# Expert stage of a two-block transformer kernel: rows turned inside gate/up, gate and residual folded into the scatter sums, last norm read from PSUM

## The reference, cut to what matters

```python
def hier_moe(h, ...):                       # t: 256 x 1024, routed to 2 of 16 experts
    def expert_step(acc, xs):
        w1e, w3e, w2e, ge = xs              # 1024x512, 1024x512, 512x1024, gate of each token
        y = (jax.nn.silu(t @ w1e) * (t @ w3e)) @ w2e
        return acc + ge[:, None] * y, None
...
x_lat = x_lat + g2 * hier_moe(h2_l, ...)    # g2: 1024 values
...
rmsnorm(x_lat, final_g)                     # y * rsqrt(mean(y*y) + eps) * g
```

## Time and profile before

| | |
|---|---|
| median of 3 runs | 1057.99 us |
| profiled execution, first to last instruction (span) | 1055.0 us |
| outside the span, against the median | 3.0 us |
| PE busy | 988.6 us (94%) |
| DVE busy | 525.0 us (50%) |
| ACT busy | 423.2 us (40%) |
| granted TensorE clock, mean over the span | 0.978 |
| bytes moved by DMA | 246.60 MB |

### The profile page before, as it was taken

One profiled execution on the slowest core, in us unless ns is written; L12 is line 12 of the kernel. 1 busy time (PEld: TensorE's weight loads), 2 busy tenths in 40 slices (PEclk: granted clock), 3 DMA queues, 4 the chain that ended last, 5 costly groups with the idle time before them and its releaser, 6 DMA issues.

```text
span 1055.0 us, 13905 instructions
## 1 busy us (share of the span) xinstructions
PE 988.6 (94%) x5609; PEld 733.3 (70%) x5609; DVE 525.0 (50%) x703; ACT 423.2 (40%) x619; POOL 154.5 (15%) x97
## 2 busy tenths in 40 slices
PE   5999999888999999999999989999999999999992
PEld 5997888665998988988798856666776444344331
DVE  5656654783665445546607516777466222212224
ACT  4446844523454334435444434565232322222111
POOL 4001000000000000000097844455000000000000
PEclk9999999988999999999999999999997999999997
DMA  9745552439644764757354522325898899999981
GB/s 306 249 146 199 199 185 95 160 123 332 221 162 160 271 235 148 264 180 255 124 169 152 182 98 80 116 85 188 319 356 331 330 421 421 422 421 421 421 362 42
DMA packets 84675, 246.60 MB, mean 234 GB/s; under 512 B 4420, under 2 KB 8283, under 8 KB 72191
## 3 DMA queue, kind: packets, MB, share of 16 engines
q1 hardware_dynamic: 82224, 240.20, 60.9%
q0 software_dynamic: 1408, 4.00, 1.4%
q10 hardware_dynamic: 974, 1.45, 0.4%
HBM read 244.59 MB, written 1.05 MB: 233 GB/s over the span
## 4 chain that ended last, share of the span: by engine, by line
PE 83%; DVE 10%; ACT 2%; issue 2%; DMA 2%; POOL 1%; SPq 0%; DVEq 0%; POOLq 0%; ACTq 0%
PE gemm_ps L1268 10%; PE gemm_ps L774 8%; PE gemm_ps L776 8%; PE gemm_ps L775 8%; PE gemm_ps L778 7%; PE gemm_ps L780 7%; PE gemm_ps L779 7%; PE gemm_ps L1309 6%; PE gemm_ps L959 2%; PE mix_ps L774 2%; PE mix_ps L775 2%; PE mix_ps L776 2%; DVE w_lo L457 2%; PE mix_ps L1319 1%; PE mix_ps L1074 1%
## 5 line engine op out<-in xcount | busy, mean ns | idle before, releaser
L451 ACT ACTIVATE w_hi<-ring 128x1024 fp32r<-128x1024 f32 (+2 forms) x222 | 227.2, 1035 | 237.1 <-PE gemm_ps L780 95.0
L457 DVE TENSOR_TENSOR w_lo<-ring,w_hi 128x1024 fp32r<-128x1024 f32 (+2 forms) x174 | 203.7, 1187 | 164.2 <-ACT w_hi L451 163.4
L778 PE MATMUL gemm_ps<-acts,w_hi 128*128 128x256 f32 x640 | 184.9, 289 | 4.1 <-DVE acts L1851 2.8
L774 PE MATMUL gemm_ps<-w_hi,acts 128*128 128x512 f32 (+2 forms) x448 | 176.6, 394 | 8.0 <-DVE w_lo L457 7.1
L779 PE MATMUL gemm_ps<-acts,w_hi 128*128 128x256 f32 x640 | 181.8, 284 | 0.0
L780 PE MATMUL gemm_ps<-acts,w_lo 128*128 128x256 f32 x640 | 181.8, 284 | 0.0
L775 PE MATMUL gemm_ps<-w_lo,acts 128*128 128x512 f32 (+2 forms) x448 | 171.9, 384 | 0.0
L776 PE MATMUL gemm_ps<-w_hi,acts 128*128 128x512 f32 (+2 forms) x448 | 171.7, 383 | 0.0
L457 POOL TENSOR_TENSOR w_lo<-ring,w_hi 128x1024 fp32r<-128x1024 f32 x48 | 122.6, 2573 | 89.1 <-ACT w_hi L451 89.1
L778 PEld LDWEIGHTS gemm_ps<-acts,w_hi 128*128 128x128 f32 x640 | 123.5, 193 | 9.5 <-issue 6.2
L779 PEld LDWEIGHTS gemm_ps<-acts,w_hi 128*128 128x128 f32 x640 | 123.5, 193 | 1.3 <-issue 1.2
(11 more groups left out here) (367 smaller groups left out, 1317.3 us busy)
## 6 DMA issues: line engine op xcount, KB each, us to landing
ring<-in_w_in_dram SPq DMA_DIRECT2D x56, 1024.0 KB, 5.0
ring<-in_w_mod_dram SPq DMA_DIRECT2D x24, 1024.0 KB, 5.7
ring<-in_w_ffn_in_dram SPq DMA_DIRECT2D x20, 1024.0 KB, 5.1
late_ring<-in_w_exp_down_dram SPq DMA_DIRECT2D x20, 1024.0 KB, 16.8
late_ring<-in_w_exp_gate_dram SPq DMA_DIRECT2D x18, 1024.0 KB, 15.7
late_ring<-in_w_exp_up_dram SPq DMA_DIRECT2D x18, 1024.0 KB, 14.0
ring<-in_w_ffn_out_dram SPq DMA_DIRECT2D x11, 1024.0 KB, 9.2
ring<-in_w_exp_up_dram SPq DMA_DIRECT2D x9, 1024.0 KB, 17.3
```

The lines of the kernel that those rows point to most:

```text
L451: nc.scalar.activation(part(w_hi, u), raw_unit(u), ACT.Copy).then_inc(hi_made, 1)
L457: eng.tensor_tensor(part(w_lo, u), raw_unit(u), part(w_hi, u), ALU.subtract).then_inc(lo_made[unit["maker"]], 1)
L774: mm(dst, xh, wh, start=a_, stop=False, skip_group_check=True)
L778: mm(dst, wh, xh, start=a_, stop=False, skip_group_check=True)
```

## The change

PE turns the hidden rows of expert `s - 1` between the two halves of `gate_and_up(s)`, no longer behind `gather`; `pick_turn` and `slot_gates` now wait until DVE has copied these rows out of the shared bank. DVE copies them at the start of its step.

The result of an expert is now made by DVE first: `DOWN` times the slot's gate times `G2`, in fp32 (`YS_RAW`, two halves, `y_scaled`); ACT copies this from SBUF as the high part; DVE subtracts the high part in place. `DOWN` is free for PE after `y_scaled`. The residual `x` is added in the same PSUM sums: PE multiplies it by the identity matrix in fp32, four products of 512 columns (`residual`), ahead of the last two `scatter` calls. DVE's two passes over the sum at the end go away, and ACT and DVE read the sum for the last norm from PSUM (`summed`), ACT for the first half of the tokens as soon as its `scatter` is done.

Step 15 and 16 are written out anew: first half of `gate_and_up(15)`, `hidden_turn(14)`, `scatter` of pair 6, second half, `pick_turn(7)`, first half of `down_product(14)`, `hidden_turn(15)`, second half, `down_product(15)` (into the bank that held gate and up of expert 14, with no wait for `y_scaled`), `residual`, the last `scatter` calls. DVE and ACT read the flag `crowded` ahead of their last results, and only the jump itself stays behind them.

```diff
         YS = ys_r[:, :].rearrange("p (h n c) -> p h n c", h=2, n=2)
+        YS_RAW = at(14336 + 2 * COL, 2, COL)
...
+        def down_bank(e):
+            return DOWN if e < NEXP - 1 else up_bank(NEXP - 2)
...
+        def summed(t):
+            return PM[:, 2 * t:2 * t + 2, :].rearrange("p b n -> p (b n)")
...
-            def gate_and_up(e):
+            def gate_and_up(e, half):
...
-                for k in range(KT):
+                for k in range(4 * half, 4 * half + 4):
...
             def pick_turn(p):
+                pe.wait_ge(sem("hidden_T"), min(2 * p + 2, NEXP - 1))
...
             def slot_gates(g):
+                if g >= 1:
+                    pe.wait_ge(sem("hidden_T"), PER_GROUP * g)
...
@@ -1290,23 +1300,25 @@
                 pe.wait_ge(sem("hidden_rows"), 2 * (e + 1))
...
-                if e % 2 == 1:
-                    pe.wait_ge(sem("pick_T"), e // 2 + 1)
+                if e == NEXP - 1:
+                    pe.wait_ge(sem("pick_T"), PAIRS)
+                elif e >= 2 and e % 2 == 0:
+                    pe.wait_ge(sem("pick_T"), e // 2)
...
-            def down_product(e):
+            def down_product(e, halves=range(2)):
                 pe.wait_ge(sem("hidden_T"), e + 1)
-                if e >= 1:
-                    pe.wait_ge(sem("y_low"), 2 * e)
-                for k in range(4):
+                if 1 <= e < NEXP - 1:
+                    pe.wait_ge(sem("y_scaled"), 2 * e)
+                for k in [2 * h + i for h in halves for i in range(2)]:
...
-                        last = mm(DOWN[half * WIN:(half + 1) * WIN, :], h, late_raw(f)[:, k % 2, half * COL:(half + 1) * COL],
+                        last = mm(down_bank(e)[half * WIN:(half + 1) * WIN, :], h, late_raw(f)[:, k % 2, half * COL:(half + 1) * COL],
...
+            def residual(t):
+                for half in range(2):
+                    mm(PM[:, 2 * t + half, :], ident, x[:, t, half * COL:(half + 1) * COL], start=False, stop=False, skip_group_check=True)
+
+            for s in range(NEXP - 1):
                 if s < 2:
                     pair_free_wait(pe, step["mod_g2"] + 2 + s)
-                if s < NEXP:
-                    gate_and_up(s)
-                if s < NEXP and s % PER_GROUP == 0:
+                gate_and_up(s, 0)
+                if s >= 1:
+                    hidden_turn(s - 1)
+                gate_and_up(s, 1)
+                if s % PER_GROUP == 0:
                     slot_gates(s // PER_GROUP)
                 if s >= 2 and s % 2 == 0:
                     pick_turn(s // 2 - 1)
...
                     if s >= 2:
-                        pe.wait_ge(sem("y_low"), 2 * (s - 1))
+                        pe.wait_ge(sem("y_scaled"), 2 * (s - 1))
                     gather(s // PER_GROUP + 1, s % PER_GROUP)
-                if s >= 1:
-                    hidden_turn(s - 1)
...
+
+            gate_and_up(NEXP - 1, 0)
+            hidden_turn(NEXP - 2)
+            for t in range(TT):
+                scatter(PAIRS - 2, t)
+            gate_and_up(NEXP - 1, 1)
+            pick_turn(PAIRS - 1)
+            down_product(NEXP - 2, (0,))
+            hidden_turn(NEXP - 1)
+            down_product(NEXP - 2, (1,))
+            down_product(NEXP - 1)
+            pe.wait_ge(sem("x_3"), 4)
+            for t in range(TT):
+                residual(t)
             for t in range(TT):
                 scatter(PAIRS - 1, t)
...
                 if s >= 1:
                     e = s - 1
-                    p, r = e // 2, e % 2 * WIN
-                    down_made_wait(act, e)
-                    if p >= 1:
-                        act.wait_ge(sem("scattered"), 2 * p)
-                    act.wait_ge(sem("slot_gates_taken"), e // PER_GROUP + 1)
+                    r = e % 2 * WIN
+                    if s == NEXP:
+                        act.wait_ge(sem("crowded_ready"), 1)
+                        again = act.value_load(crowded[0:1, 0:1], min_val=0, max_val=1)
                     for half in range(2):
-                        b = slice(half * WIN, (half + 1) * WIN)
-                        A(YS[r:r + WIN, 0, half, :], DOWN[b, :], ACT.Copy, scale=SLOT_GATES[r:r + WIN, e:e + 1]).then_inc(sem("y_high"), 1)
-            act.wait_ge(sem("crowded_ready"), 1)
-            again = act.value_load(crowded[0:1, 0:1], min_val=0, max_val=1)
+                        act.wait_ge(sem("y_scaled"), 2 * e + half + 1)
+                        A(YS[r:r + WIN, 0, half, :], YS_RAW[r:r + WIN, half, :], ACT.Copy).then_inc(sem("y_high"), 1)
...
                     A(SL[:, 0, :], PG[:, 0, :], ACT.Silu).then_inc(sem("rest_silu"), 1)
-            act.wait_ge(sem("x_4"), 2)
-            norm_squares("last", x, JUNK3)
+                act.wait_ge(sem("rest_summed"), TT)
+            for t in range(TT):
+                act.wait_ge(sem("scattered"), 2 * PAIRS - 1 + t)
+                j = 2 * NORM["last"] + t
+                A(JUNK3, summed(t), ACT.Square, accum_out=ss[:, j:j + 1]).then_inc(squares, 1)
+                act.wait_ge(squares, j + 1)
...
+            def hidden_copy(e):
+                dve.wait_ge(sem("hidden_turned"), e + 1)
+                V_.tensor_copy(HIDDEN[:, e % 2].rearrange("p j q -> p (j q)"), TURNED[:, 0:2 * P]).then_inc(sem("hidden_T"), 1)
+
+            def pick_copy(p):
+                dve.wait_ge(sem("pick_turned"), p + 1)
+                if p >= 1:
+                    dve.wait_ge(sem("scattered"), 2 * p)
+                V_.tensor_copy(PICK_T, TURNED[:, 0:SEQ]).then_inc(sem("pick_T"), 1)
+
             for s in range(NEXP + 1):
+                if 1 <= s < NEXP:
+                    hidden_copy(s - 1)
...
-                if s >= 2 and s % 2 == 0:
-                    p = s // 2 - 1
-                    dve.wait_ge(sem("pick_turned"), p + 1)
-                    if p >= 1:
-                        dve.wait_ge(sem("scattered"), 2 * p)
-                    V_.tensor_copy(PICK_T, TURNED[:, 0:SEQ]).then_inc(sem("pick_T"), 1)
+                if s == NEXP - 1:
+                    pick_copy(PAIRS - 1)
+                elif s >= 2 and s % 2 == 0 and s < NEXP:
+                    pick_copy(s // 2 - 1)
                 if s < NEXP:
...
                 if s >= 1:
                     e = s - 1
                     p, rows_ = e // 2, slice(e % 2 * WIN, (e % 2 + 1) * WIN)
-                    dve.wait_ge(sem("hidden_turned"), e + 1)
-                    V_.tensor_copy(HIDDEN[:, e % 2].rearrange("p j q -> p (j q)"), TURNED[:, 0:2 * P]).then_inc(sem("hidden_T"), 1)
+                    if s == NEXP - 1:
+                        hidden_copy(NEXP - 1)
+                    if s == NEXP:
+                        dve.wait_ge(sem("crowded_ready"), 1)
+                        again = dve.value_load(crowded[0:1, 0:1], min_val=0, max_val=1)
+                    down_made_wait(dve, e)
+                    if p >= 1:
+                        dve.wait_ge(sem("scattered"), 2 * p)
+                    dve.wait_ge(sem("slot_gates_taken"), e // PER_GROUP + 1)
+                    for half in range(2):
+                        V_.scalar_tensor_tensor(YS_RAW[rows_, half, :], down_bank(e)[half * WIN:(half + 1) * WIN, :], SLOT_GATES[rows_, e:e + 1],
+                                                G2[rows_, half * COL:(half + 1) * COL], ALU.mult, ALU.mult).then_inc(sem("y_scaled"), 1)
                     for half in range(2):
                         dve.wait_ge(sem("y_high"), 2 * e + half + 1)
-                        V_.scalar_tensor_tensor(YS[rows_, 1, half, :], DOWN[half * WIN:(half + 1) * WIN, :], SLOT_GATES[rows_, e:e + 1],
-                                                YS[rows_, 0, half, :], ALU.mult, ALU.subtract).then_inc(sem("y_low"), 1)
+                        V_.tensor_tensor(YS[rows_, 1, half, :], YS_RAW[rows_, half, :], YS[rows_, 0, half, :], ALU.subtract).then_inc(sem("y_low"), 1)
...
-            dve.wait_ge(sem("crowded_ready"), 1)
-            again = dve.value_load(crowded[0:1, 0:1], min_val=0, max_val=1)
             with dve.If(again == 1):
...
                     if e == NEXP - 1:
                         rest_link(V_.tensor_tensor(REST_ACC, REST_ACC, G2, ALU.mult))
-                        rest_link(V_.tensor_tensor(x[:, t, :], x[:, t, :], REST_ACC, ALU.add))
-
-            for t in range(TT):
-                dve.wait_ge(sem("scattered"), 2 * PAIRS - 1 + t)
-                link(V_.tensor_tensor(XN3[:, t, :], PM[:, 2 * t:2 * t + 2, :].rearrange("p b n -> p (b n)"), G2, ALU.mult))
-                V_.tensor_tensor(x[:, t, :], x[:, t, :], XN3[:, t, :], ALU.add).then_inc(sem("x_4"), 1)
+                        dve.wait_ge(sem("scattered"), 2 * PAIRS - 1 + t)
+                        V_.tensor_tensor(summed(t), summed(t), REST_ACC, ALU.add).then_inc(sem("rest_summed"), 1)
+                        dve.wait_ge(sem("rest_summed"), t + 1)
...
                 inv_sqrt(V_.tensor_scalar(r, sq, 1.0 / D, EPS, ALU.mult, ALU.add))
```

(12 more changed lines are left out.)

## The result

The changed kernel takes 1049.83 us (median of 4 runs, 1049.16 to 1050.50), the kernel before 1058.09 us beside it: ratio 0.9918, 95% interval 0.9900 to 0.9936. It is faster, by 8.3 us. I had forecast 1047.7 with a range of 1044.5 to 1052.2, so the direction and the range held; the time is 2.1 above the forecast, and 8.3 of the forecast 10.3 us came. The 3.0 us that I put around the span are 1.8 in the four runs of after (1050.50 against 1048.7 in the profiled one), and 1.8 to 1.9 in all 38 later executions of before that have both numbers.

The account below looks back on a forecast made before the run. PE was taken to set the pace, with the weight loads 2.9 us ahead. Span 1055.0 - 3.7 (last expert, including 0.3 lost in the steps) - 6.6 (tail) = 1044.7, plus 3.0 around the span: 1047.7 us, range 1044.5 to 1052.2.

Parts of the forecast that it names:

- Steps 1 to 14, the turn: Turn moved into the middle of gate/up: 0.4 us each, 3.7 saved in steps 12 and 14, 0.3 lost in all.
- Hidden work of DVE and ACT: Steps 1 to 14: two extra DVE operations per expert, some 3.2 us of result work, hidden behind 7 us of gate/up.
- The last expert: Step 15 to last scatter: no PE wait, full clock in down_product(15), scatter starts at 1035.05 instead of 1038.72, 3.7 saved.
- Residual: Four fp32 products ahead of the last scatter, 3.44 us; PE ends last by 0.35, about the residual's net cost.
- Tail: Last scatter to last normed row: four DVE passes of 1.23 go, 13.2 us becomes 6.5, 6.6 saved.
- the jump: Tail: ACT's jump over unused code, with its last copy; at worst 0.7 us late, taken as zero.
- The wall: Weight loads of expert 15 land 2.9 us before PE begins it, limiting what shorter steps 1 to 14 can pay.
- The rival of the lower end: Weights become the wall if the inserted turn costs nothing; gain over forecast stops at 3.2, 1044.5 us; chance 0.10.
- no landing moves: Loads are queued 24 to 26 us, so places freed earlier or later move no landing; last load at 1026.4.
- Around the span: 3.0 us between the profiled span of 1055.0 and the median of 1057.99, assumed to stay, added to 1044.7.

Follow-up runs that it names:

- fold_only: Kernel before in its old order, with only gate, G2 and residual folded into the sums and the last norm read from PSUM; 1053.43 us, ratio 0.9949.
- fold_again: Second profile, no edit, of the kernel before with only the folding added and the old order kept; 1053.76 us, ratio 0.9951.
- half_scatter: Changed kernel, turns inside gate/up only from step 12, scatters of pairs 0 to 5 without the low part (timing only); 1049.30 us, ratio 0.9913.
- residual_early: Changed kernel, turns inside gate/up only from step 12, residual products moved to steps 4, 6, 8, 10; 1045.90 us, ratio 0.9885.
- both_early: Changed kernel, turns inside gate/up only from step 12, residual in steps 4, 6, 8, 10, DVE/ACT jump ahead of step 15; 1047.25 us, ratio 0.9885.
- order_only: Changed kernel with the old way of making results (ACT first, from PSUM), no residual, old tail; 1056.27 us, ratio 0.9974.

## Why the prediction was right, point by point

- *Steps 1 to 14, the turn.* Direction right, size off, and this is the term that was mis-sized: 0.4 taken, 0.52 measured. I composed 0.10 + 0.14 + 0.10. The way in is the 0.10 (957.26 to 957.79 is 0.53, as in the earlier trace rows); two transposes and the way back take 0.37, not 0.24, and the first block then 0.05 more. The 0.14 of the earlier trace rows was the distance to the scatter's record, which starts too early by the overlap found above. In steps 3, 5, 7, 9 and 11 the turn's old place gives back 0.24 to 0.28 and not 0.14, so these steps lose the 0.26 of the forecast: two errors of 0.12 cancel there, which is luck. Steps 12 and 14 saved 1.60 and 1.43, 3.0 together, where I had 3.7, because the picking turn, too, must now change back before the down product (0.34 and 0.37 instead of 0.2) and the turn costs more. Six steps lose 0.51 to 0.55, 3.1 in all (2.4 forecast), six lose 0.24 to 0.37, 1.7 in all (1.6 forecast); with the 3.0 saved that is the 1.74 between the marks, against 0.3. It is 1.4 of the 1.9 us that are missing in the stage.
- *Hidden work of DVE and ACT.* Right: PE waits nowhere in the steps for results, and the scatter of pair 6 has no wait. The two profiles of the folding alone show what the cover is worth at the last expert, 0.7 us of longer wait and the fallen clock.
- *The last expert.* Right about the clock and the missing wait. That the size agrees so closely (20.38 against 20.35) is luck. The picking turn took 0.37 and the hidden turn 0.36 instead of 0.2 and 0.24, the halves of `down_product(14)` 1.87 and 1.77 instead of 1.8 and 1.7, 0.43 in all; my own terms add up to 1034.9 and not to 1035.05; and the scatter's record starts 0.30 early. Without the last, the stretch is about 20.7, 0.3 over the forecast, and the step that failed is again the price of a turn. The clock fell here in all three profiles in which PE waits 2.5 to 3.2 us for DVE (before, fold_only, fold_again). In the others this wait is gone and the clock stays up until the last scatter, but for half_scatter, where it fell behind the wait for weights. Removing the wait paid its length and the 1.7 us of the slow products.
- *Residual.* Right: PE ends behind the results, by 0.1 us in the records and by about 0.4 with the overlap, where I had 0.35. That with it the clock stays up where a wait of 3.0 us let it fall, I hadn't seen.
- *Tail.* The four passes went as forecast, and from the first row's final pass to the end it is 3.30 as in the sum. 0.4 were missing at the beginning, and not for the reason I had ready (the jump): 0.30 of them are the overlap of two records, time that belongs to the last expert. ACT starts 2.18 ahead of DVE's pass instead of 2.08. The 2.94 us that I took from DVE as the price of ACT's jump are too much: ACT starts 2.34 us behind the end of its last copy with the jump between them, and there it waits for the scatter.
- *The wall.* The rival of the lower end was right about where the wall stands: I had 2.9 us of room in before, and kernels with less work for PE begin step 15 at 193.3 to 194.3, 1.7 to 2.6 us ahead of before's 195.97. It played no part in the changed kernel because the turn cost too much to reach it. That no landing moves was only nearly so: the same load lands at 193.1 in before, at 194.1 in both profiles of the changed kernel and at 193.1 to 194.3 in the rest, and the last load, forecast at 1026.4, came at 1029.5, 1.0 us later when both are counted from the first block.
- *Around the span.* 3.0 taken, 1.8 to 1.9 in every run of either kernel that shows it. The other 1.2 us are that the profiled execution of before was quicker than the median: 1055.0 is as short as the shortest span among the 38 later executions (1055.0 to 1062.0). The term was named wrongly and still gave the right sum. The in-stage difference of 8.4 and the measured 8.3 agree without it.

## What to carry to other kernels

Fill a wait where there is one, and leave a step alone whose wait is ended by someone else: moving the turn paid 3.0 us in steps 12 and 14 and cost 4.4 in steps 1 to 11. When an edit frees the bound engine, compare first with the landing of the last loads; here a kernel 4 us better stood exactly at it, and 5.3 us more of freed work came back as waits and a slower clock. And a wait removed just ahead of long products can be worth more than its length, and one added there can cost more, if the clock falls behind it; whether it does has to be read from the clock of each profile.

## What the runs showed of the hardware

- A turn of two 128 x 128 fp32 blocks between products that run two to the array costs 0.52 us in all. Among instructions of the full array the same turn costs 0.24 to 0.28, by what steps 3 to 11 gave back for it. The rest, for two changes of arrangement, is about 0.13 us for each, an estimate from these two numbers. That agrees with the drain at a change of tiling mode of the Trainium skill (TensorEngine Tiling, Key Properties).
- The clock fell to the lower level behind waits of PE of 2.3 us (half_scatter), 3.0 us (residual_early, both_early), 3.2 us (fold_only, fold_again) and 2.5 us (before), and behind the two waits of 0.8 and 0.9 us in step 12 of the folding alone, in both of its profiles. It stayed up in the one profile of before with the same two waits, behind the waits of 2.35 us ahead of the last scatter of before and order_only, and behind those of 1.6 and 1.1 us in half_scatter. So the length of the wait alone doesn't tell. Each fall cost 1.1 to 1.7 us.
- The record of a product can start before the product has the array: the scatter's starts 0.30 us early behind the residual, and 0.1 us early behind two transposes, so a distance between starts across two kinds of instruction can be too short by that much.
- PE's first product began 0.24 us behind the landing of its load in all six profiles in which it had run up to the loads (0.24 to 0.25).
- Reading 1024 fp32 columns from PSUM took ACT 1.03 us with a sum of squares, from SBUF 1.06.
